# A Strassen-like encoder kernel: two of four weight sums made by adding transfers instead of by VectorE

## The reference, cut to what matters

```python
for layer in range(2):
    h = rms_norm(x, mix_norm_g[layer])
    x = x + (conv_attention_mixer(h, ...) if layer % 2 == 0 else short_conv_mixer(h, ...))
    h = rms_norm(x, ffn_norm_g[layer])
    x = x + (silu(h @ w_gate) * (h @ w_up)) @ w_down
# short_conv_mixer: bg, cg, u = split(h @ w_in, 3); (bg * conv3(cg * u)) @ w_out
```

## Time and profile before

| what | value |
|---|---|
| median of 3 runs | 2091.77 us (2089.01 to 2093.17) |
| the profiled execution, its own time | 2090.54 us |
| its span, first to last instruction | 2088.7 us |
| PE busy | 2061.8 us, 99% of the span |
| DVE busy | 1463.3 us, 70% |
| ACT busy | 1113.8 us, 53% |
| POOL busy | 472.6 us, 23% |
| moved by DMA | 394.30 MB, mean 189 GB/s |

### The profile page before, as it was taken

How to read it: one execution, slowest core, us unless ns; L and a number is a source line. 1 busy time by engine, 2 the same in 40 slices (tenths; PEclk the granted TensorE clock), 3 DMA queues, 4 the chain that set the end, 5 groups by cost and what they waited for, 6 DMA issues and landing times.

```text
span 2088.7 us, 24352 instructions
## 1 busy us (share of the span) xinstructions
PE 2061.8 (99%) x9598; PEld 1718.1 (82%) x9598; DVE 1463.3 (70%) x1468; ACT 1113.8 (53%) x1265; POOL 472.6 (23%) x260
## 2 busy tenths in 40 slices
PE   9998999999999999999999999999999999999999
PEld 8888778888888888888888888888888888888887
DVE  5787879955887358873776884578738983389832
ACT  6677566544555445554554554455545554455542
POOL 3676730022000420014211014400140003300033
PEclk9999999999999999999999999999999999999999
DMA  7533455556565565645666455566465555655554
GB/s 252 159 124 112 145 198 181 180 180 215 183 225 175 184 213 194 235 153 181 210 212 196 160 192 189 179 214 231 152 230 193 180 192 189 236 181 182 192 192 161
DMA packets 208450, 394.30 MB, mean 189 GB/s; under 512 B 11344, under 2 KB 21968, under 8 KB 208336
## 3 DMA queue, kind: packets, MB, share of 16 engines
q1 hardware_dynamic: 207760, 392.21, 55.2%
q10 hardware_dynamic: 576, 0.53, 0.1%
HBM read 390.60 MB, written 2.10 MB: 188 GB/s over the span
## 4 chain that ended last, share of the span: by engine, by line
PE 91%; issue 3%; DVE 3%; ACT 2%; POOL 1%; DMA 0%; SPq 0%; DVEq 0%; ACTq 0%; POOLq 0%
PE pair L664 12%; PE pair L666 12%; PE pair L665 12%; PE pair L745 11%; PE pair L747 11%; PE pair L746 11%; PE pair L732 6%; PE pair L730 6%; PE pair L731 6%; PE tbank L760 2%; DVE pair L1754 1%; POOL cv L630 1%; DVE w_lo L1597 1%; ACT w_hi L1168 1%; PE pair L811 0%
## 5 line engine op out<-in xcount | busy, mean ns | idle before, releaser
L1168 ACT ACTIVATE w_hi<-w_raw 128x1024 fp32r<-128x1024 f32 x584 | 616.9, 1059 | 609.4 <-PE pair L666 324.3
L1597 DVE TENSOR_TENSOR w_lo<-w_raw,w_hi 128x1024 fp32r<-128x1024 f32 x425 | 539.0, 1270 | 397.5 <-ACT w_hi L1168 397.2
L618 POOL TENSOR_TENSOR w_lo<-w_raw,w_hi 128x1024 fp32r<-128x1024 f32 x159 | 387.2, 2436 | 1600.9 <-ACT w_hi L1168 1600.8
L745 PE MATMUL pair<-w_hi,xT_hi 128*128 128x512 f32 x1040 | 404.7, 389 | 0.4 <-DVE w_lo L1597 0.4
L747 PE MATMUL pair<-w_hi,xT_lo 128*128 128x512 f32 x1040 | 404.8, 389 | 0.0
L746 PE MATMUL pair<-w_lo,xT_hi 128*128 128x512 f32 x1040 | 404.6, 389 | 0.0
L1168 ACT ACTIVATE w_hi<-s_raw 128x1536 fp32r<-128x1536 f32 x182 | 270.9, 1488 | 183.9 <-PE pair L747 124.2
L1597 DVE TENSOR_TENSOR w_lo<-s_raw,w_hi 128x1536 fp32r<-128x1536 f32 x182 | 318.2, 1759 | 63.3 <-ACT w_hi L1168 63.3
L664 PE MATMUL pair<-w_hi,yT_hi 128*128 128x512 f32 x704 | 274.8, 390 | 0.0
L666 PE MATMUL pair<-w_hi,yT_lo 128*128 128x512 f32 x704 | 274.1, 389 | 0.0
L665 PE MATMUL pair<-w_lo,yT_hi 128*128 128x512 f32 x704 | 273.9, 389 | 0.0
(11 more groups left out here) (198 smaller groups left out, 2565.9 us busy)
## 6 DMA issues: line engine op xcount, KB each, us to landing
w_raw<-in_w_down SPq DMA_DIRECT2D x176, 512.0 KB, 4.3
w_raw<-in_w_up SPq DMA_DIRECT2D x110, 512.0 KB, 6.0
w_raw<-in_w_gate SPq DMA_DIRECT2D x110, 512.0 KB, 3.7
w_raw<-in_sc_in SPq DMA_DIRECT2D x72, 512.0 KB, 4.3
s_raw<-in_w_gate SPq DMA_DIRECT2D x44, 768.0 KB, 8.0
s_raw<-in_w_up SPq DMA_DIRECT2D x44, 768.0 KB, 7.6
w_raw<-in_w_in SPq DMA_DIRECT2D x52, 512.0 KB, 4.1
w_raw<-in_w_out SPq DMA_DIRECT2D x32, 512.0 KB, 3.5
```

Source lines behind the costliest of these rows:

```text
L618: nc.gpsimd.tensor_tensor(w_lo[at], raw(o), w_hi[at].bitcast(F32), ALU.subtract).then_inc(w_lo_pool, 1)
L745: nc.tensor.matmul(b, x_hi(k, t), w_hi[:, r, kk, :], start=(first[t] and kk == 0), stop=False)
L1168: nc.scalar.activation(w_hi[:, o % RING, tiles_of(o), :], raw(o), ACT.Copy).then_inc(w_hi_ready, 1)
L1597: nc.vector.tensor_tensor(w_lo[at], raw(o), w_hi[at].bitcast(F32), ALU.subtract).then_inc(w_lo_dve, 1)
```

## The change

Two of the four remakes go. The first sum, T1 = G0 + U0, is made by loading U0 into place 2 and then beginning a second transfer that adds G0 to it in SBUF (`first_sum`). The third, U4 + U0, is made by a transfer that adds U0 to U4 in place 1 (`third_sum`), after operand 1 has used U4 and after the remaining DVE sum has read it. Both are begun by POOL, with `accum_op=ALU.add`. The two DVE sums left are place 0 = place 1 + place 2 (operand 6) and place 3 = place 3 + place 0 (operand 12). Operand 3 reads place 2 and waits for `t_added[0]`, operand 9 reads place 1 and waits for `t_added[1]`. Since a transfer can only add, the signs of the sums move to the activations' side (three small sums for each norm) and to `up_sums`, which now subtracts.

SP no longer loads U0 as a unit's third block. `first_block` loads it for the next unit ahead of time: behind the rest operand o + 11 of the unit before, or ahead of the last four loads of the job before. G0 and U0 are therefore read twice from HBM.

```diff
-PRODUCT_PLACES = {0: 0, 1: 1, 3: 0, 5: 3, 6: 0, 9: 2, 12: 3}
-MADE = {3: 1, 6: 2, 9: 3, 12: 4}
+PRODUCT_PLACES = {0: 0, 1: 1, 3: 2, 5: 3, 6: 0, 9: 1, 12: 3}
+MADE = {6: 1, 12: 2}
+ADDED = {3: 0, 9: 1}
@@ SP
+            def first_block(name):
+                n, _, _ = UNIT[name]
+                if n:
+                    sp.wait_ge(t_made, 2 * n - 1)
+                    low_done(sp, UNIT_BASE[n - 1] + 3)
+                s_block(2, columns(name)[1], 0)
...
                 if n:
-                    sp.wait_ge(t_made, 4 * n)
+                    sp.wait_ge(t_made, 2 * n)
                     low_done(sp, UNIT_BASE[n - 1] + 6)
-                block(0, gates, 0)
-                block(1, ups, 4)
-                rest(o + 2, ups, 0)
+                s_block(0, gates, 0)
                 if n:
                     low_done(sp, UNIT_BASE[n - 1] + 9)
-                block(2, ups, 0)
+                s_block(1, ups, 4)
+                rest(o + 2, ups, 0)
                 rest(o + 4, ups, 1)
...
                 rest(o + 11, ups, 3)
+                if name_after is not None:
+                    first_block(name_after)
                 rest(o + 13, ups, 4)
@@ POOL
+            def first_sum(name):
+                n, o, _ = UNIT[name]
+                pool.wait_ge(s_loaded[2], 16 * (n + 1))
+                nc.gpsimd.dma_start(s_raw[:, 2, :, :], columns(name)[0][:, 0:SK, :],
+                                    accum_op=ALU.add).then_inc(t_added[0], 16)
+
+            def third_sum(name):
+                n, o, _ = UNIT[name]
+                low_done(pool, o + 1)
+                pool.wait_ge(t_made, 2 * n + 1)
+                nc.gpsimd.dma_start(s_raw[:, 1, :, :], columns(name)[1][:, 0:SK, :],
+                                    accum_op=ALU.add).then_inc(t_added[1], 16)
+
+            def down_lows(first, last, name_after):
+                for o in range(first, last):
+                    if o == last - 4 and name_after is not None:
+                        first_sum(name_after)
+                    if ON_POOL[o]:
+                        low(o)
@@ DVE, unit
                 lows(at, o + 2)
-                dve.wait_ge(s_loaded[2], 16 * (n + 1))
-                remake(n, 1, 0, 2, 0)
                 lows(o + 2, o + 3)
...
-                dve.wait_ge(t_made, 4 * n + 1)
-                remake(n, 2, 0, 1, 0)
+                dve.wait_ge(t_added[0], 16 * (n + 1))
+                remake(0, 1, 2)
                 if before is not None:
                     lows(o + 4, o + 5)
                 lows(o + 5, o + 7)
-                dve.wait_ge(t_made, 4 * n + 2)
-                remake(n, 3, 2, 1, 2)
                 lows(o + 7, o + 8)
```

More of the change, by code:

```diff
@@ L406, in encoder_kernel @@
         t_made = sem("t_made")
+        t_added = [sem(f"t_added{i}") for i in range(2)]
         snapped = sem("snapped")
@@ L540, in _, with s_block, columns, unit @@
                 load_job(JOB[("conv_out", nb)][0], w_out, 0, SH, nb * NB)
[L542 removed]
+            def s_block(place, view, k0):
+                sp.dma_start(s_raw[:, place, :, :], view[:, k0:k0 + SK, :]).then_inc(s_loaded[place], 16)
+            def first_block(name):
[4 more added lines that the diff above has]
+                s_block(2, columns(name)[1], 0)
+            def columns(name):
+                layer, i = name
+                if layer == "sc":
+                    view = sc_in.rearrange("(k p) n -> p k n", p=P)
+                    return view[:, :, ds(i * NB + D, NB)], view[:, :, ds(i * NB + 2 * D, NB)]
+                return (w_gate[layer].rearrange("(k p) n -> p k n", p=P)[:, :, ds(i * NB, NB)],
+                        w_up[layer].rearrange("(k p) n -> p k n", p=P)[:, :, ds(i * NB, NB)])
+            def unit(name, name_after=None):
                 n, o, _ = UNIT[name]
[L546 to L547 removed]
+                gates, ups = columns(name)
                 def rest(o, view, q):
@@ L565, in unit @@
                     low_done(sp, UNIT_BASE[n - 1] + 12)
-                block(3, gates, 4)
+                s_block(3, gates, 4)
                 rest(o + 7, gates, 0)
@@ L638, in _, with columns, ffn @@
                 add_taps(products_by(s - 2), products_by(s))
-            for o in range(first_ffn, SLOTS):
-                if ON_POOL[o]:
-                    low(o)
+            def columns(name):
+                layer, i = name
+                if layer == "sc":
+                    view = sc_in.rearrange("(k p) n -> p k n", p=P)
+                    return view[:, :, ds(i * NB + D, NB)], view[:, :, ds(i * NB + 2 * D, NB)]
+                return (w_gate[layer].rearrange("(k p) n -> p k n", p=P)[:, :, ds(i * NB, NB)],
+                        w_up[layer].rearrange("(k p) n -> p k n", p=P)[:, :, ds(i * NB, NB)])
+            def first_sum(name):
[15 more added lines that the diff above has]
+                        low(o)
+            def ffn(layer):
+                for ch, (u0, u1) in enumerate(CHUNKS):
+                    for i in range(u0, u1):
+                        third_sum((layer, i))
+                        if i + 1 < u1:
+                            first_sum((layer, i + 1))
+                    after = (layer, u1) if u1 < NF else ("sc", 0) if layer == 0 else None
+                    down_lows(JOB[("down", layer, ch, 0)][0], JOB[("down", layer, ch, NJ - 1)][0] + chunk_slots(ch), after)
+            first_sum((0, 0))
+            ffn(0)
+            for j in range(NJ):
+                third_sum(("sc", j))
+                s0 = JOB[("bg", j)][0]
+                down_lows(s0, s0 + SD, ("sc", j + 1) if j + 1 < NJ else None)
+            s0 = JOB[("sc_out", 0)][0]
+            down_lows(s0, s0 + NJ * SD, (1, 0))
+            ffn(1)
         @block.tensor
@@ L1991, in _, with remake @@
                     x_split(1, nb)
-            def remake(n, step, dest, a, b):
+            def remake(dest, a, b):
                 nc.vector.tensor_tensor(s_raw[:, dest, :, :], s_raw[:, a, :, :], s_raw[:, b, :, :],
-                                        ALU.subtract).then_inc(t_made, 1)
+                                        ALU.add).then_inc(t_made, 1)
             def bank_sum(dest, bank, source):
@@ L2060, in unit @@
                 if norm is None:
-                    remake(n, 4, 3, 3, 0)
+                    dve.wait_ge(t_made, 2 * n + 1)
+                    remake(3, 3, 0)
                 dve.wait_ge(w_used, o + 7)
```

45 lines of the change are left out of this document (30 added, 15 removed).

## The result

| | before | after |
|---|---|---|
| median | 2090.62 us (4 runs) | 2124.49 us (4 runs, 2120.92 to 2124.55) |
| the profiled execution's span | 2088.7 us | 2122.7 us |
| first matmul of the first unit | 315.42 | 312.42 |
| from there to the end of the span | 1773.3 us | 1810.3 us |

The change is slower: ratio 1.0154, 95% interval 1.0138 to 1.017. The forecast of "the same, 2091" is wrong. The time lies inside the range, near the smaller of the two prices of the rival "third sum late" (2116).

A forecast was written before the change was run, and what follows sets the result against it. PE was taken to bound the kernel everywhere but around the first unit. 2090.54 us less 0.55 gained there, all other terms 0, gave 2090.0; with 1.23 for the runs' median, 2091. Range 2088 to 2148.

The forecast's parts named there:

- third sum late: Rival, chance 0.34: POOL's slow start makes the third sum's transfer take 10.9 us, each unit waits 0.95 us: 2116; at 12.1, 2148.
- What bounds the kernel: PE never waits from 324.10 to 2084.00 us, so DVE's 91 us saved are worth nothing outside the first unit.
- The gain of 0.55 us in the first unit: PE's wait at operand 2 goes, 0.55 us, provided the first sum has landed when ACT begins operand 3.
- Signs: Small sums per norm and unit change operation, not size or number: cost 0.
- first sum: 26 adding transfers, wanted by operand 3 of the next unit, 22 us of cover inside a chunk: cost 0.
- POOL's turns at a job's end: In 9 places the first sum precedes POOL's low parts; POOL may be held 7.4 us before PE waits: cost 0.
- traffic: 41 MB more on top of 394, tightest in the burst at a chunk's start: cost 0.
- The third sum: Before operand 9: PE waits only if the transfer takes over 9.9 us from the remake's end; estimated 8.5, cost 0.
- 1.0 + 3.9 + 3.3 + 0.3 = 8.5: Third sum's transfer in us: start, its bytes counted twice, SP's competing loads, notice.
- The cross-check: Third sum's transfer another way: median landing 7.9 us plus 1.96 for the second read, 9.9 us.
- POOL shut out by DVE: Rival, chance 0.07: POOL's start of the third sum waits out DVE's low parts, about 4.5 us: 13.0 us, total 2171.
- Low parts late at a job's end: Rival, chance 0.05: POOL takes 10 us over a first sum, 2.6 us lost in 9 places: 23 us, 2114.

The follow-up runs named there:

- run 1: Changed kernel with the third sum made by a DVE instruction instead of an adding transfer: 2088.78 us, ratio 0.999 to before.
- run 6: Changed kernel with SP's next-unit block begun after operand 13's load and DVE's bank sum moved ahead: 2093.88 us, ratio 1.0013 to before.
- run 7: As run 6, and in the first unit alone DVE makes the third sum instead of a transfer: 2090.34 us, ratio 1.0007 to before.
- run 4: Changed kernel with the third sum's transfer plain, without the addition, overwriting place 1: 2093.67 us, ratio 1.0012 to before.
- run 5: Changed kernel with DVE adding operand 6's bank before operand 9's low part and the last remake: 2097.47 us, ratio 1.0029 to before.
- run 3: Changed kernel with SP's load of the next unit's first block moved behind operand 13's load: 2096.88 us, ratio 1.0034 to before.

## Why the prediction was wrong

**What bounds the kernel: right.** PE does, outside the first unit. Less busy DVE brought nothing: 80 us less in the change, 35 in run 1, 75 and 74 in runs 6 and 7.

**The gain of 0.55 us in the first unit: there, and mostly given back.** The wait of 0.55 us at operand 2 is gone. But the condition was missed: ACT took the first sum 5.3 us into the unit (317.68), where I wanted it by 3.9. I had 9.9 us for the sum; from POOL's start (306.44) to ACT it took 11.2. Operand 3 begins 8.59 us into the unit, against 8.74 before and 8.03 in run 1, where the first sum landed sooner (ACT 4.3 us into the unit). The 0.6 us by which run 1 is ahead are this gain. The late first sum had a further price, below.

**Signs, first sum, POOL's turns at a job's end, traffic: right, 0.** Run 1 contains them all and is not slower.

**The third sum: the limit right, the estimate failed.** "PE waits when the transfer takes more than 8.3 + 1.67 = 9.9 us from the remake's end, and then one for one". It measures 22.01 − 5.60 − 6.34 = 10.07 us in an ordinary unit (operand 9's place, the way from ACT's copy to it, the remake's end), and the chain of waits ran over the bank sum as described. The sum "1.0 + 3.9 + 3.3 + 0.3 = 8.5" is what failed, and in it the first term, the "1.0 us of start". The whole was 10.87. Windows of that unit show when bytes begin to move (columns as above):

```profile
610.50:611.00 0.50, 0.50 (x4) 0.42 (x3) 0.50 (x1) 0.50 (x1) 0.21 (x1) 1.00 0.00 0
611.00:611.50 0.50, 0.50 (x4) 0.42 (x3) 0.50 (x1) 0.09 (x1) 0.00 (x0) 1.00 1.47 106
```

The view of the queues shows whose bytes they are, first from the remake's end (608.88) to 613.38, then from there to 619.75, when ACT starts:

```profile
q1 hardware_dynamic: 209, 0.43, 47.1%
...
q0 software_dynamic: 400, 0.79, 66.8%
q1 hardware_dynamic: 484, 0.94, 41.9%
```

- *Start, taken at 1.0 us, is 4.5.* POOL begins 0.55 us behind the remake and its instruction lasts 1.28 us. The first packet of its queue (q0) moves 2.7 us after that, at 613.4. What moves from 611.0 on is SP's load of operand 11, begun at 610.05: 0.43 MB of it pass first. I had taken the start of a plain transfer that SP issues with nothing beside it.
- *Movement and notice, taken at 3.9 + 3.3 + 0.3 = 7.5 us, are 6.4* (613.38 to 619.75). The company that I counted was there, but part of it had passed during the start. The doubling was right: 0.786 MB counted twice and the 0.8 MB of loads beside it make 5.9 us at 401 GB/s, an estimate; from the first to the last packet of the sum it is 6.0 us.

The cross-check in the prediction gave 9.9, from the median landing of a burst. I set it aside since "only two transfers compete". It was nearer to 10.87, but not for a reason: no term in it stands for a start of 4.5 us.

**Two terms were not there at all.** One limit does not hold for 26 units. Where a chunk begins, no work of a unit before stands ahead of operand 9: PE is there 21.08 us into the unit, and the remake ends at 6.72. The limit is 21.08 − 5.60 − 6.72 = 8.8 us, only 0.3 above my estimate. In the second units of an FFN the remake ends at 7.40, and the limit is 9.0. And in the very first unit the remake ends 11.3 us in and not 6.5, and operand 9 was late by 4 us. Most of that is this unit's own order: in it DVE makes the low part of operand 4 ahead of the remake, and before the change the second remake ended 10.7 us in as well. The late first sum added about 1 us: in runs 4 and 5, where ACT took it 4.2 us into the unit, the remake ended at 10.3. In exchange the last units of a chunk, with no block of a next unit beside them, did not wait, but for one of 0.2 us. The other term is the clock: four of the waits cost more than one for one. 5.8 us of half speed came on top of 27.5 us of waits.

**The rivals.** "Third sum late", at a chance of 0.34, is what happened, with the right place and way: 2116 us against 2124. That its 10.9 us per transfer meets the 10.87 measured is luck. It put 2.4 us, the time of one of POOL's low parts, on top of the 1.0, a start of 3.4 us where 4.5 were measured, and kept 7.5 us for movement and notice where 6.4 were; the two errors cancel. The difference between 2116 and 2124 is the two terms just told. It had all 26 units wait 0.95 us; 17 waited 1.6 us on average. "POOL shut out by DVE" did not come: POOL began its instruction at 609.43, 0.55 us behind the remake, while DVE ran low parts without a gap, and it lasted 1.28 to 1.30 us there as in every other unit. The sentence of the Trainium skill that spoke against it (SBUF — State Buffer, "Who interferes with whom") agrees with that, if beginning a transfer reads nothing in SBUF, which no row shows. "Low parts late at a job's end" did not come either.

**How the chances should have stood.** Between an estimate of 8.5 and a limit of 9.9 us there were 1.4 us. The start of 1.0 us was that of another engine's plain transfer, and the rival's 2.4 us more for POOL were enough to pass the limit by 1.0. With a cross-check that fell on the limit itself the late sum deserved more than half.

## What to carry to other kernels

Handing work from an idle-enough engine to a transfer pays nothing when that engine was not waited for, and it changes a step of 1.75 us into one of 8 to 13: look for the place with the shortest time between what the step needs and who needs it, and work out its limit in every kind of unit, the first one and the seams too. An estimate that is inside such a limit by less than its unknown terms is not "the same". Count a transfer's start to the first packet of its own queue, and ask which loads are begun just ahead of it: here that was the term furthest off, and it had been taken from another engine's transfer. If the transfer must stay, first take out what stands between its landing and the engine that sets the time (run 5: an independent sum ahead of the dependent low part, worth 27 us) and what runs beside it (run 3, 28 us); each moved only a few lines.

## What the runs showed of the hardware

**A transfer that adds in SBUF takes the queues for nearly twice the time per byte.** The queues in the profile of the change, SP's plain loads (q1) and POOL's additions (q0), with packets, MB and share of 16 engines:

```profile
q1 hardware_dynamic: 207760, 392.21, 54.6%
q0 software_dynamic: 20800, 40.90, 11.0%
```

11.0% of 2122.7 us are 233 us for 40.90 MB; 54.6% are 1159 us for 392.21 MB. Per byte that is 1.93 times. In the last unit of a chunk, where the addition runs alone for a while, the windows show the same at full share:

```profile
659.50:660.00 0.50, 0.50 (x4) 0.41 (x3) 0.50 (x1) 0.50 (x1) 0.00 (x0) 1.00 1.13 209
```

209 GB/s, against 401 for plain loads. The Trainium skill (Collectives: The Full Stack, part 3) gives half the rate to a transfer that reduces, because two sources are read through one ring; the trace agrees for an addition in SBUF, with 0.52. That the second read is the reason, no run here shows by itself. It is the addition and not POOL's queue: the rows of q0 in run 1 (first sums only, all adding) and in run 4 (the same and the third transfers plain) are

```profile
q0 software_dynamic: 10400, 20.45, 5.5%
...
q0 software_dynamic: 15808, 40.90, 8.6%
```

5.5% of 2091.1 us are 115 us for the first sums. Take these from the 180 us of run 4 (8.6% of 2089.5) and 65 us are left for 20.45 MB of plain transfers from POOL, an estimate, near the 60 us that SP's loads take for as many bytes.

**Beginning a transfer costs POOL 1.28 us with an addition and 0.80 without**, median over the transfers of 768 KB; a plain one from SP stands at 0.47 to 0.48 us in the trace. **How soon a transfer's first packet follows depends on what else is begun at about that time.** In 14 of the change's 52 adding transfers (10 first sums inside chunks, the 4 third sums of the short convolution) SP begins no load within 2 us of POOL's start on either side, and the first packet came 0.7 us after POOL's instruction. In the other 38 SP begins one from 1.6 us ahead to 1.1 us behind, and it came 1.5 to 4.5 us after.

**A wait can cost more than its length.** The spells at 1.2 GHz behind four of the 17 waits added a fifth to what the waits themselves took. The length of a stop alone does not say whether such a spell follows: run 6 has stops of 1.2 and 2.3 us in its first unit and no matmul at the lower level from there on, while in run 4 one stop of 2.1 us at the same place was followed by seven matmuls 0.43 us apart.
